# Two of the memory attention's value chunks made in the last step of the first attention

## The reference

```
mix = concat([nsa_mixer(...8 heads...), pool_mixer(...), sgu_mixer(...)]) @ w_out
x = x + rms_norm(mix)
h = rms_norm(x);  m = rms_norm(mem)            # mem: 256 tokens, does not depend on x
x = x + rms_norm(memory_attention(h, m, w_mq, w_mk, w_mv, w_mo))   # 4 heads of 256
```

## Time and profile before

| | |
|---|---|
| median of 3 runs | 988.83 us (988.73 to 989.19) |
| the profiled execution | 988.69 us, its span 987.0 us |
| TensorE busy | 959.2 us, 97% of the span |
| VectorE busy | 675.6 us, 68% |
| ScalarE busy | 545.7 us, 55% |
| granted TensorE clock, mean | 0.998 of full |
| DMA | 159.04 MB, mean 161 GB/s |

### The profile page before, as it was taken

One profiled execution on the slowest core, in us unless ns is written; L12 is line 12 of the kernel. 1 busy time (PEld: TensorE's weight loads), 2 busy tenths in 40 slices (PEclk: granted clock), 3 DMA queues, 4 the chain that ended last, 5 costly groups with the idle time before them and its releaser, 6 DMA issues. The chain is left out here.

```text
span 987.0 us, 20761 instructions
## 1 busy us (share of the span) xinstructions
PE 959.2 (97%) x7813; PEld 921.4 (93%) x7813; DVE 675.6 (68%) x1054; ACT 545.7 (55%) x838; POOL 124.6 (13%) x131
## 2 busy tenths in 40 slices
PE   7999899999899999999999999999999999999997
PEld 7998789999899999998999999999999989999886
DVE  5788857454699987446877777766675448668743
ACT  5867466456689965554444444444463426654733
POOL 2100010001044453000111111101100000000000
PEclk9999999999999999999999999999999999999999
DMA  8743334435255556661655555555455434334551
GB/s 325 253 143 120 117 108 143 157 108 171 65 192 192 190 192 204 202 198 59 201 173 176 173 172 172 172 187 171 155 173 185 144 114 146 96 122 151 192 177 57
DMA packets 45223, 159.04 MB, mean 161 GB/s; under 512 B 6083, under 2 KB 7107, under 8 KB 44908
## 3 DMA queue, kind: packets, MB, share of 16 engines
q1 hardware_dynamic: 44668, 156.61, 48.5%
q0 software_dynamic: 496, 1.59, 0.5%
HBM read 157.11 MB, written 1.06 MB: 160 GB/s over the span
## 5 line engine op out<-in xcount | busy, mean ns | idle before, releaser
L1533 DVE TENSOR_TENSOR w_lo<-raw,w_hi 128x1024 fp32r<-128x1024 f32 x290 | 357.2, 1237 | 135.8 <-ACT w_hi L550 135.5
L550 ACT ACTIVATE w_hi<-raw 128x1024 fp32r<-128x1024 f32 x290 | 304.6, 1054 | 115.4 <-PE acc L1040 86.7
L1038 PE MATMUL acc<-AH,w_hi 128*128 128x256 f32 (+1 forms) x832 | 238.9, 287 | 0.9 <-DVE AL L1554 0.9
L1040 PE MATMUL acc<-AH,w_lo 128*128 128x256 f32 (+1 forms) x832 | 236.4, 284 | 0.0
L1039 PE MATMUL acc<-AL,w_hi 128*128 128x256 f32 (+1 forms) x832 | 236.3, 284 | 0.0
L1038 PE MATMUL acc<-XH,w_hi 128*128 128x256 f32 (+1 forms) x664 | 192.4, 290 | 7.7 <-DVE w_lo L1533 3.3
L1040 PE MATMUL acc<-XH,w_lo 128*128 128x256 f32 (+1 forms) x664 | 189.1, 285 | 0.0
L1039 PE MATMUL acc<-XL,w_hi 128*128 128x256 f32 (+1 forms) x664 | 188.8, 284 | 0.0
L1038 PEld LDWEIGHTS acc<-AH,w_hi 128*128 128x128 f32 x832 | 157.8, 190 | 2.6 <-DVE AL L1554 1.1
L1040 PEld LDWEIGHTS acc<-AH,w_lo 128*128 128x128 f32 x832 | 157.8, 190 | 0.0
L1039 PEld LDWEIGHTS acc<-AL,w_hi 128*128 128x128 f32 x832 | 157.5, 189 | 0.1
(11 more groups left out here) (365 smaller groups left out, 1378.0 us busy)
## 6 DMA issues: line engine op xcount, KB each, us to landing
raw<-weights SPq DMA_DIRECT2D x290, 512.0 KB, 3.5
cst<-params SPq DMA_DIRECT2D x1, 1195.0 KB, 6.1
XR<-x_t SPq DMA_DIRECT2D x2, 512.0 KB, 5.8
Y<-mem_t SPq DMA_DIRECT2D x1, 1024.0 KB, 9.7
AR<-bias_rows POOLq DMA_DIRECT2D x4, 256.0 KB, 5.4
out<-AR SPq DMA_DIRECT2D x2, 512.0 KB, 3.0
AR<-final_gain POOLq DMA_DIRECT2D x1, 512.0 KB, 3.6
AR<-onehot SPq DMA_DIRECT2D x1, 66.0 KB
```

Of the source, the lines that this page charges most:

```text
L550: nc.scalar.activation(w_hi[:, n % SLOTS, :], raw[:, n % SLOTS, :], ACT.Copy).then_inc(hi_ready, 1)
L1038: nc.tensor.matmul(o, wh, h, start=start, stop=False)
L1040: return nc.tensor.matmul(o, wl, h, start=False, stop=stop)
L1533: V.tensor_tensor(w_lo[:, s, :], raw[:, s, :], w_hi[:, s, :].bitcast(F32), ALU.subtract).then_inc(lo_ready, 1)
```

## The change

The last four value chunks are split. The pair for head 2 (`mva`) is put ahead of `w_out` in the stream and made in step 7 of the first attention, between `pv(6)` and `turn(7)`; ACT copies it right after the gating unit's Gelu. The pair for head 3 (`mvb`) stays in the memory attention, now behind `m_pv(1)`. The number of chunks, products and copies is the same. Because the stream has two chunks more ahead of `w_out`, ACT and DVE no longer skip their two conversions in step 7, and the tile numbers behind `mva` move by one, to the other bank.

```diff
-           ("pool", 2), ("mk", 8), ("sgu_mix", 0), ("pool_mix", 0), ("w_out", 8), ("mv", 4), ("mq", 8), ("mv2", 4),
+           ("pool", 2), ("mk", 8), ("sgu_mix", 0), ("mva", 2), ("pool_mix", 0), ("w_out", 8), ("mv", 4), ("mq", 8), ("mvb", 2),
...
+            def v_act(h, last):
+
+                wait_chunk(act, last)
+                t = value_tile(h)
+                freed(nc.scalar.activation(VM[:, 2 * h:2 * h + 2, :, :].rearrange("p r b c -> p b r c"),
+                                           acc(t)[:, :].rearrange("p (b r c) -> p b r c", b=2, r=2), ACT.Copy), t)
...
                     nc.scalar.activation(uT[:, :, :], uT[:, :, :], ACT.Gelu_apprx_tanh).then_inc(sgu_gelu, 1)
+                    v_act(2, CHUNK["mva"] + 1)
...
-                if h < HEADS - 1:
-                    ahead(n + 1)
+                ahead(n + 1)
...
-            ahead(CHUNK["mv2"])
+            ahead(CHUNK["mvb"])
             m_exp(3)
-            v_act("mv2", 0)
             m_hi(1)
-            ahead(CHUNK["mv2"] + 1)
-            ahead(CHUNK["mv2"] + 2)
+            ahead(CHUNK["mvb"] + 1)
+            v_act(3, CHUNK["mvb"] + 1)
             m_copy(2)
-            v_act("mv2", 1)
-            ahead(CHUNK["mv2"] + 3)
             m_copy(3)
...
                     sgu_products()
                     pv(h - 1)
+                    pair_tokens(CHUNK["mva"], TILE["mva"], mem_h, mem_l)
                 turn(h)
...
             m_qk(3)
-            pair_tokens(CHUNK["mv2"], TILE["mv2"], mem_h, mem_l)
             m_pv(1)
+            pair_tokens(CHUNK["mvb"], TILE["mvb"], mem_h, mem_l)
             m_turn(2)
-            pair_tokens(CHUNK["mv2"] + 2, TILE["mv2"] + 1, mem_h, mem_l)
             m_turn(3)
```

More of the change, by code:

```diff
@@ L44 @@
     NCHUNKS += _n
-_TILES = dict(sgu_v=1, cmp=1, vsw=1, sgu_mix=1, pool_mix=2, mv=2, mv2=2, down=8, conv_out=8, lout=2)
+_TILES = dict(sgu_v=1, cmp=1, vsw=1, sgu_mix=1, pool_mix=2, mv=2, mva=1, mvb=1, down=8, conv_out=8, lout=2)
 TILE = {}
@@ L345, in wide_acc, with value_tile @@
             return acc(TILE[name] + r)[:, 0:w] if r < 2 else SC[:, (r - 2) * 512:(r - 2) * 512 + w]
+        def value_tile(h):
+            return TILE["mv"] + h if h < 2 else TILE[("mva", "mvb")[h - 2]]
         def up_acc(r):
@@ L695, in fill_act @@
                     nc.scalar.activation(rs2, mv[:, :, 1], ACT.Sqrt, bias=eps_col).then_inc(sgu_root, 1)
+            def v_act(h, last):
[3 more added lines that the diff above has]
+                                           acc(t)[:, :].rearrange("p (b r c) -> p b r c", b=2, r=2), ACT.Copy), t)
             for h in range(HEADS):
                 n = CHUNK["sgu_v"] + 2 * h
-                if h < HEADS - 1 and h != GELU_HEAD + 1:
+                if h != GELU_HEAD + 1:
                     ahead(n)
@@ L743, in _ @@
                 to_y(t, m, "g_mix_post", n)
[L745 to L750, removed]
             take_root(NORM_MIX, S, loaded=True)
@@ L758, in mv_fill @@
                 if q == 2:
-                    v_act("mv", 0)
+                    v_act(0, CHUNK["mv"] + 1)
             to_hi_and_square(META, 0, "g_mem_pre", mv_fill)
@@ L763, in _ @@
             take_root(NORM_X1, S, loaded=True)
-            v_act("mv", 1)
+            v_act(1, CHUNK["mv"] + 3)
             ahead(CHUNK["mv"] + 3)
@@ L1332, in m_pv @@
                 pe.wait_ge(m_copied, h + 1)
-                t = TILE[("mv", "mv2")[h // 2]] + h % 2
-                wait_evacuated(pe, t)
+                wait_evacuated(pe, value_tile(h))
                 if h >= 2:
@@ L1933, in _ @@
             m_lo(1)
-            for c in range(1, 4):
-                ahead(CHUNK["mv2"] + c)
+            ahead(CHUNK["mvb"] + 1)
             m_lo(2)
@@ L2214, in _pack_weights @@
     mv = lin(a["w_mv"][0])
-    parts += lin(a["w_mk"][0]) + lin(a["w_out"][0]) + pairs_of("mv", mv[0:4]) + lin(a["w_mq"][0]) + pairs_of("mv2", mv[4:8])
+    parts += lin(a["w_mk"][0]) + pairs_of("mva", mv[4:6]) + lin(a["w_out"][0]) + pairs_of("mv", mv[0:4])
+    parts += lin(a["w_mq"][0]) + pairs_of("mvb", mv[6:8])
     parts += lin(a["w_mo"][0])
```

## The result

The changed kernel takes 991.86 us (median of 9 runs, 991.18 to 993.03) against 989.10 (988.71 to 990.28) for the kernel before in the same rounds: 1.0026 times as long, 95% interval 1.0016 to 1.0037. Slower by some 2.6 us, on the far side of the 0.2% named above; 991.2 was forecast.

What follows compares the result with a forecast made beforehand. TensorE, busy 959.2 of 987.0 us, was taken to bound the kernel through its work, gaps and clock. +4.4 us in step 7 less 2.0 in the memory attention gave +2.4, 991.2 us, range 989.3 to 992.7.

Steps and rivals of the forecast that it cites:

- Step 7: First attention: the pair closes the 3.87 us gap, but a 2.9 us wait opens before the pooling products; +4.4 us.
- The conversion of chunk 1: Step 7: w_lo of w_out chunk 1 adds 1.22 us ahead of the reciprocal, costed at nothing because the pair covers it.
- The lower bound: Step 7 with the clock staying up: block 4 of w_out moves by 3.6 to 3.7 us, against 4.8 otherwise.
- Memory attention: Second place: 5.9 us of pair work leaves, new waits open, and mo starts 2.0 us earlier.
- The two waits: Memory attention: PE waits 2.2 us for m_copy(1) before m_pv(1) and 1.6 us for m_copy(2) before m_pv(2).
- rival 3: Memory attention: the clock falls a second time after the 2.2 us wait, 1.7 us more, 992.9 us; chance 0.12.
- The sum: Whole kernel: +4.4 in the first attention less 2.0 in the memory attention, +2.4 us, 991.2 us.
- Rival 1: First attention: the clock stays up after the new 2.9 us gap; sum +1.65 us, 990.4 us; chance 0.27.
- rival 2: Both attentions: a waiting instruction holds up nothing behind it, so the change is faster; -5.2 us, 983.6 us; chance 0.06.

Runs made afterwards that it cites:

- e1: The changed kernel with chunk 2 of w_out rounded on ScalarE after head 7's transposes' copy and finished on VectorE after the last mixing result: 988.08 us.
- e1a: The changed kernel with only VectorE's w_lo of w_out's chunk 2 moved after the last mixing result, ScalarE's order left as in the change: 987.55 us.
- e2b: The changed kernel with head 3's pair ahead of m_pv(1), and on ScalarE the values' copy and mo chunk 2's rounding ahead of m_hi(1): 988.28 us.
- e5: The kernel before with m_pv(1) ahead of the first late pair, m_hi(1) ahead of the pair's copy, and no chunk moved: 991.82 us, ratio 1.0028.
- e4: The changed kernel with 7 idle products of 128 columns between turn(7) and the pooling products: 991.00 us, ratio 1.0015.
- e3: The changed kernel with w_out chunk 2's conversion late on both engines, head 3's pair ahead of m_pv(1), and ScalarE's values' copy and rounding ahead of m_hi(1): 984.23 us.
- e2: The changed kernel with only PE's order changed in the memory attention, the pair ahead of m_pv(1): 989.60 us, ratio 1.0009.
- e6: The kernel before with 14 idle products of 128 columns behind pv(6), after head 7's scores are read: 987.65 us, ratio 0.9983.

## Why the prediction was right

The step that it rests on, that in-order queues on VectorE and ScalarE turn into new waits of PE, is shown by e1, e1a, e2b and e5.

**Step 7.** `turn(7)` was forecast for 126.7 and came at 126.83, the pooling products for 130.4 and came at 130.65 (less 0.16: 130.5). The wait was forecast at 2.9 us from issue to issue; in these terms it was 3.2 (3.00 of idleness), since the transposes took less than the 0.8 us counted for them. The conversion of chunk 1 cost nothing, as costed. The clock fell, which was taken over the rival that it stays up, and its price was mis-sized: +4.4 was put between bounds of 3.6 and 4.8, the profiled execution shows 4.9, since the low stretch lay over the pooling products and most of `pv(7)` as before. `w_out` starts at 134.49, just behind the 132.5 to 134.3 that were named. The lower bound is borne out by e4, where the clock stayed up: 14.47 less 10.59 is 3.9. Undoing the conversion's place gave 4.0 us by the traces, 3.8 by the medians (991.86 to 988.08).

**Memory attention.** The two waits were forecast at 2.2 and 1.6 us of issue; the trace shows 1.89 and 1.31 of idleness, which is the same less 0.3 us for the last product's end. 2.0 us were to be won. In the profiled execution the stretch from block 4 to `mo` is 0.7 us shorter than before (87.07 against 87.72). In e1a, with the same order there and no fall of the clock, it is 85.57: 2.15 us won, which bears the term out. The second fall, rival 3, took the rest. It need not be in every execution: the eight others, at a mean clock of 0.997 or 0.998, are 0.8 to 1.9 us shorter. They are known by time and mean clock only; 0.998 is also the mean of the kernel before, with its one fall. The forecast gave it 0.12 against the forecast's 0.45, too little: 1.9 us of idleness were "far from 3.87" and yet enough in three of the five traces that have this wait (the change, e1, e4).

**The sum.** The 2.4 forecast is 2.6 by the ratio and 2.8 by the medians. The terms are +4.9 and, without a second fall, -2.15 (e1a), together 2.7; the profiled execution, with it, has 4.9 - 0.7 = 4.2. Part of the closeness of the sum is luck: both terms were too small, and they have opposite signs. Rival 1 (clock up) fell with the windows; rival 2 (a waiting instruction holds up nothing) fell with the 2.68 us that VectorE idled in front of its conversion; it would have been 983.6, and e3, which takes the waits away by order, reaches 984.23. That the move is good and only the order around it spoilt it was not said in the prediction; e3 shows it.

The Trainium skill's page "TensorE: Matmul & The Clock Gate" (section "Architectural detail: the array is 16× 32×32, not 1× 128×128") says that ScalarE and VectorE queues are strict FIFO. The trace agrees: L1821 waited 2.68 us and a conversion behind an instruction that was not ready. The same page of the Trainium skill has a section "HAM oscillation — how this bites in real kernels", by which short gaps would leave the clock up. The measurements here differ from it, and they decide: after 3.0 us of idleness the clock fell, after 1.9 us it fell in three of five traces (the change, e1, e4; not e1a, e5), after 1.73 us in e2's memory attention and after 1.43 us in e4's step 7, behind products without use, it did not.

What stays open: why the clock of an execution falls or does not after 1.9 us of idleness. That was not tried further.

## What to carry to other kernels

Work that fills a gap brings its own conversions and copies along, and what decides is where these stand in the queues of the other engines: put them behind whatever PE will wait for next, even where they "only" keep a pipeline of weights ahead. Before a filler is taken from a place, look at what is late there without it, and leave a piece that covers it. Count a gap of some 2 us or more on TensorE at its length and, if the clock falls, 1 to 2 us more (1.0 in step 7 by the change and e4, 1.7 in the memory attention by e1 and e1a, 2.1 in e5's step 7 against e6's); where no useful filler exists, products without use can pay.

## What the hardware showed that was not expected

The spread of the run times has two sources that the traces show: the clock, and the start. With no gap over 1.5 us behind the kernel's first, five runs lay within 0.35 us (e3), but e6, of which the same is true, spread over 1.2 us in eleven; e1, whose only long gap is 1.9 us, has two groups some 1.8 us apart, which fits the 1.7 us of a fall. The start of `pv(6)` differs by 1.3 us between e5 and e4 (119.73, 121.01) without any fall ahead of it; 1.0 of it is there already among the kernel's first weight chunks, one of which starts at 11.98 and at 13.00.

A fall does not even need a long gap. In e2's profiled execution the clock went down at 56.5 us for 3.4 us, with 0.34 us of idleness in front; the other nine traces have the same products there at full speed. Rows of its timeline, and a window (its clock is the 0.50):

```profile
53.86 1.86 PE L1175 MATMUL turned<-AR 128*128 128x32 f32 x16
56.07 0.30 PE L1180 MATMUL outs<-ident,AR 24*128 24x24 f32 x2 [0.34 <-ACT AR L672]
56.30 1.51 PE L1223 MATMUL scores<-AR 64*128 64x128 f32 x8
...
57.00:59.00 2.00, 2.00 (x10) 1.35 (x9) 1.33 (x3) 0.00 (x0) 0.00 (x0) 0.50 0.48 145
```

From the first of these lines to `pv(6)` it took 67.74 us there and 66.06 in e2b, 1.7 us less. That accounts for e2's profiled execution lying 1.6 us above its median.

A gap of the same length can also cost more from one execution to the next. Windows of e5's profiled execution, around the gap of 3.86 us in step 7 that it shares with the kernel before:

```profile
118.00:123.00 5.00, 2.60 (x33) 1.98 (x32) 3.91 (x9) 2.77 (x10) 0.00 (x0) 1.00 0.35 107
123.00:130.00 7.00, 5.54 (x26) 3.11 (x26) 4.39 (x13) 2.78 (x4) 0.00 (x0) 0.54 0.00 0
```

Here the clock fell within the gap and stayed low for some 6.8 us (a mean of 0.54 over 7 us), where that of the kernel before was low for 3.4 us; the transposes at 124.46 already ran at half speed. Block 4 came 11.71 us behind the start of `pv(6)` in place of 10.59; with the clock up it was 9.57 (e6), so the clock cost 2.1 us here and 1.0 there.
